# One level of Strassen's scheme in the MLP of a two-block model kernel, in two phases with sums that pass through DRAM

## The reference, cut to what matters

```
h  = h + m @ w_o                                   # [1024, 1024]
hn = rms_norm(h, norm2_g)
gate, up = split(hn @ w_gate_up)                   # w_gate_up [1024, 2 * 2816]
x  = rms_norm(h + (silu(gate) * up) @ w_down, final_g)   # w_down [2816, 1024]
h2 = rms_norm_2(x, pre_norm_g)                     # the second block goes on from here
```

## Time and profile before

| | |
|---|---|
| median of 3 runs | 2475.63 us (2475.03 to 2477.4) |
| span of the profiled execution | 2474.4 us |
| TensorE busy, mean granted clock | 2305.9 us (93%), 0.971 |
| VectorE, ScalarE, GpSimd busy | 1235.1, 774.9, 804.8 us |
| bytes moved by DMA | 135.97 MB, mean 55 GB/s |

### The profile page before, as it was taken

One profiled execution on the slowest core, in us unless ns is written; L12 is line 12 of the kernel. 1 busy time (PEld: TensorE's weight loads), 2 busy tenths in 40 slices (PEclk: granted clock), 3 DMA queues, 4 the chain that ended last, 5 costly groups with the idle time before them and its releaser, 6 DMA issues.

```text
span 2474.4 us, 30540 instructions
## 1 busy us (share of the span) xinstructions
PE 2305.9 (93%) x11208; PEld 1902.4 (77%) x11208; DVE 1235.1 (50%) x2685; ACT 774.9 (31%) x1327; POOL 804.8 (33%) x380
## 2 busy tenths in 40 slices
PE   6999999999997789999899999999999789998896
PEld 6876788988885677878688888888888577787875
DVE  3368899999304678220433333333333544506723
ACT  5245422332224455022411111111111442226632
POOL 1355433555432121223432222323232532230032
PEclk9999999999998799999999999999999799999998
DMA  3211112111132000422111111111111031110122
GB/s 104 58 52 65 55 43 56 52 35 52 52 98 65 26 9 1 168 62 78 35 52 42 51 42 51 42 51 46 48 51 43 26 120 52 43 43 22 54 71 85
DMA packets 178082, 135.97 MB, mean 55 GB/s; under 512 B 4529, under 2 KB 163918, under 8 KB 177982
## 3 DMA queue, kind: packets, MB, share of 16 engines
q1 hardware_dynamic: 173990, 121.48, 16.4%
q10 hardware_dynamic: 3992, 13.11, 1.3%
HBM read 116.87 MB, written 16.78 MB: 54 GB/s over the span
## 4 chain that ended last, share of the span: by engine, by line
PE 74%; DVE 8%; ACT 3%; POOL 2%; issue 2%; DMA 0%; ACTq 0%; DVEq 0%; POOLq 0%
PE ps L705 27%; PE ps L914 19%; PE ps L931 9%; PE ps L977 8%; PE ps L1123 3%; PE ps L813 2%; PE ps L834 2%; PE ps L846 2%; DVE logit L1768 1%; ACT p_s L1582 1%; POOL n_acc L2318 1%; DVE logit L1755 1%; PE ps L871 1%; POOL x_lo L2346 1%; PE ps L1046 0%
## 5 line engine op out<-in xcount | busy, mean ns | idle before, releaser
L2137 POOL TENSOR_TENSOR w_lo<-w_raw,w_hi 128x1024 fp32r<-128x1024 f32 (+1 forms) x127 | 276.1, 2175 | 898.9 <-ACT w_hi L1155 898.9
L705 PE MATMUL ps<-x_hi,w_hi 128*128 128x512 f32 (+2 forms) x1200 | 455.4, 379 | 8.3 <-DVE c_rs L1673 3.3
L705 PE MATMUL ps<-x_lo,w_hi 128*128 128x512 f32 (+2 forms) x1200 | 452.4, 377 | 0.0
L705 PE MATMUL ps<-x_hi,w_lo 128*128 128x512 f32 (+2 forms) x1200 | 450.4, 375 | 0.0
L2294 POOL TENSOR_TENSOR w_lo<-w_raw,w_hi 128x1024 fp32r<-128x1024 f32 x66 | 158.9, 2408 | 504.0 <-ACT w_hi L1444 504.0
L914 PE MATMUL ps<-x_hi,w_hi 128*128 128x512 f32 x704 | 277.9, 395 | 2.5 <-POOL x_lo L2278 2.5
L914 PE MATMUL ps<-x_lo,w_hi 128*128 128x512 f32 x704 | 279.1, 396 | 0.0
L914 PE MATMUL ps<-x_hi,w_lo 128*128 128x512 f32 x704 | 277.5, 394 | 0.0
L705 PEld LDWEIGHTS ps<-x_hi,w_hi 128*128 128x128 f32 x1200 | 228.0, 190 | 52.7 <-issue 11.5
L705 PEld LDWEIGHTS ps<-x_hi,w_lo 128*128 128x128 f32 x1200 | 227.8, 190 | 37.2
L705 PEld LDWEIGHTS ps<-x_lo,w_hi 128*128 128x128 f32 x1200 | 227.7, 190 | 36.2
(11 more groups left out here) (341 smaller groups left out, 4075.4 us busy)
## 6 DMA issues: line engine op xcount, KB each, us to landing
w_raw<-in_w_in SPq DMA_DIRECT2D x74, 512.0 KB, 3.7
w_raw<-in_w_gate_up SPq DMA_DIRECT2D x44, 512.0 KB, 3.8
w_raw<-in_w_down SPq DMA_DIRECT2D x22, 512.0 KB, 3.5
q_scratch<-stage ACTq DMA_DIRECT2D x8, 512.0 KB, 2.6
g_scratch<-g_ring ACTq DMA_DIRECT2D x8, 512.0 KB, 2.7
q_f<-q_scratch SPq DMA_DIRECT2D x8, 512.0 KB, 4.1
w_raw<-in_w_b SPq DMA_DIRECT2D x8, 512.0 KB, 5.0
g_s<-g_scratch SPq DMA_DIRECT2D x8, 512.0 KB, 3.7
```

Of the source, the lines that this page charges most:

```text
L705: mm = pe.matmul(ps[:, b, 0:n], w[:, s, P * k:P * k + P], r[:, k, t0:t0 + n], start=k == 0 and i == 0, stop=k == kd - 1 and i == 2 and ext ...
L2137: pool.tensor_tensor(w_lo[:, p % 2, 0:n], w_raw[:, p % 2, 0:n], w_hi[:, p % 2, 0:n], ALU.subtract).then_inc(wlo_done, 1)
```

## The change

The MLP is done in two phases. Activations and weights are cut in halves: activations by model width (m 0 to 3, m 4 to 7) and by token half, the gate and up panels of a chunk by model width, so that gate and up for both token halves are a 2x2 by 2x2 block product. One level of Strassen's scheme (in Winograd's form) makes it from seven products P1 to P7 in place of eight; a product is one 128x512 bank, 4 k-steps of 3 matmuls.

Phase 1: `strassen_pair(n)`, n from 0 to 21, with 84 matmuls each. VectorE makes the weight sums (`combined_weights`, 4 instructions per chunk), the output sums (`gate_up_pair`, 5) and, in every second pair, sums of two chunks' inner activations (`inner_sums`, 4). GpSimd makes sums of the down weights (`down_combined`, 4 per two chunks). Inner sums (7 x 256 KB per two chunks) and down-weight sums (4 x 256 KB) are stored to DRAM. The residual `mix` is stored to DRAM as `h_scratch` (4 MB), since its place holds the normalised activations and their sums; VectorE waits for these stores (`hs_store`) before it normalises in place.

Phase 2: `down_step(s)`, s from 0 to 76: seven products (p) of 11 steps (j), each with 12 matmuls into four banks. Each step loads 256 KB of weights and 256 KB of inner activations, ScalarE casts both, VectorE and GpSimd take one low part each. Banks change sides with each product, and `down_sums` and `with_residual` sum the seven into `mix`. `h_scratch` is loaded back from step 14 on. Squares for the next norm are taken for finished tiles from the fifth product on; four tiles of 128x512 are left for the end.

The loops of the MLP are written out instead of being loops of the chip. The diff, cut to its core:

```diff
             def norm_sums(i):
-                pe.wait_ge(acca_done, 7 * i + 7)
                 if i:
-                    pe.wait_ge(accb_done, 7)
-                    pe.wait_ge(upper_free, 2 * KD + 16 * (FC - 1))
+                    pe.wait_ge(acc2a_done, 14)
+                    pe.wait_ge(acc2b_done, 14)
+                    pe.wait_ge(dn_done, 28)
+                else:
+                    pe.wait_ge(acca_done, 7)
...
-            def gate_and_up(it, par, first=False, between=None):
-            def down(it, par, off, chunks=1):
...
+            def strassen_pair(n):
+                at = 4 * (n % 2)
+                for i, prod in enumerate(products(n)):
+                    q = 7 * n + i
+                    pe.wait_ge(*low_w(q))
+                    if prod == "P2":
+                        pe.wait_ge(r1_done, n + 1)
+                    if prod == "P7":
+                        pe.wait_ge(po_done, 5 * n + 1)
+                    if prod == "P3":
+                        pe.wait_ge(po_done, 5 * n + 3)
...
+                    b = at + {"P1": 0, "P2": 0, "P6": 1, "P7": 1, "P5": 2, "P3": 2, "P4": 3}[prod]
+                    for k in range(4):
+                        if n == 0:
+                            pe.wait_ge(*low_x(4 * i + k))
+                        for e, (w, r) in enumerate(((wr_hi, xb_hi), (wr_hi, xb_lo), (wr_lo, xb_hi))):
+                            mm = pe.matmul(ps[:, b, :], w[:, q % SLOTS, P * k:P * k + P], r[prod][:, k, :],
...
+            def down_step(s):
+                p, j = s // HJ, s % HJ
+                pe.wait_ge(*low_w(M2 + s))
+                pe.wait_ge(*low_s(s))
+                for f in range(4):
...
+                    for e, (w, r) in enumerate(((wr_hi, sr_hi), (wr_hi, sr_lo), (wr_lo, sr_hi))):
+                        mm = pe.matmul(ps[:, 4 * (p % 2) + f, :], w[:, (M2 + s) % SLOTS, P * f:P * f + P], r[s % SLOTS][:, :],
...
+            sp.wait_ge(h_done, 2 * KD)
+            load_pair(1)
+            for m in range(KD):
+                sp.dma_start(h_scratch[m], mix[:, m, :]).then_inc(hs_store, 16)
...
+            for s in range(STEPS):
...
+                if s >= 4:
+                    sp.wait_ge(*low_w(M2 + s - 4))
+                sp.dma_start(block_source(M2 + s), down_weights(p, j)).then_inc(wst_load[s % 4], 16)
...
+                if s >= 4:
+                    sp.wait_ge(*low_s(s - 4))
+                if s == 8:
+                    store_inner(HJ - 1)
...
+                sp.dma_start(wdr[:, s % 4, :], as_scratch[p, j]).then_inc(sst_load[s % 4], 16)
+                if 14 <= s < 14 + KD:
...
+                    sp.dma_start(mix[:, s - 14, :], h_scratch[s - 14]).then_inc(h_load, 16)
...
+            dve.wait_ge(hs_store, 16 * KD)
+            for z in range(8):
+                normalized(z)
+            for y in (1, 3):
+                x_low(y)
...
+            def gate_up_pair(n):
+                if n + 1 < FC:
+                    combined_weights(n + 1)
+                for i in range(7):
+                    if i == at("P6"):
...
+                        dve.tensor_tensor(a[0][:, :], r1[:, :], ps[:, b + 1, :], ALU.add).then_inc(po_done, 1)
+                    if i == at("P7"):
...
+                        dve.tensor_tensor(g1[:, :], r1[:, :], ps[:, b + 1, :], ALU.add).then_inc(po_done, 1)
+                        dve.wait_ge(po_done, done + 2)
+                        dve.tensor_tensor(a[1][:, :], g1[:, :], ps[:, b + 2, :], ALU.add).then_inc(po_done, 1)
...
+                    block_low(q + SLOTS)
+                    if i == 2 and n >= 2 and n % 2 == 0:
+                        inner_sums(n // 2 - 1)
...
+            def block_high(q):
...
+                    act.wait_ge(tw_done, TW_DONE_0 + 4 * n + 4)
+                if q >= SLOTS:
+                    act.wait_ge(blk_done, BLK_DONE_0 + q - SLOTS + 1)
+                act.copy(wr_hi[:, q % SLOTS, :], block_source(q)).then_inc(wh_done, 1)
...
+            def final_squares(z):
+                m, h = FINAL[z]
+                act.wait_ge(dn_done, 9 + z if z < 4 else 11 + 2 * (z - 3) if z < 8 else 13 + z)
+                for st in range(2):
+                    if z >= 3:
+                        act.wait_ge(acc2b_done if st else acc2a_done, added(z - 2))
+                    dst = n_acc2[:, st, half(h)] if z in (0, 4) else n_sq2[st][:, z % 2, :]
+                    act.activation(dst, mix[:, m, half(h)], ACT.Square, scale=v("final_g", m) if st else 1.0).then_inc(sq2_done, 1)
```

More of the change, by code:

```diff
@@ L954, in _ @@
             pe.wait_ge(h_done, 2 * KD)
-            gate_and_up(0, 0, first=True)
-            with pe.Fori(0, (FC - 2) // 2) as it:
-                for par in range(2):
-                    gate_and_up(it, par + 1)
-                    down(it, par, 3 * par + 4)
-            it_last = (FC - 2) // 2
-            gate_and_up(it_last, 1, between=memory_turned)
+            for n in range(FC):
+                strassen_pair(n)
+            for s in range(STEPS):
+                down_step(s)
+                if s == 6 * HJ + 4:
+                    memory_turned()
             pe.wait_ge(memlo_done, MEMLO_0 + KD)
-            down(it_last, 0, 4, chunks=2)
             def linear(key, j, rhs_hi, rhs_lo, t0, n):
@@ L1473, in _ @@
-            it_last = (FC - 2) // 2
-            activations(it_last, 1, between=memory_high_parts)
-            for m in range(KD):
-                act.wait_ge(upper_free, 2 * KD + 16 * (FC - 2) + 2 * m + 2)
-                squares(1, m)
-            split_mlp(it_last, 6, L2)
-            split_mlp(it_last, 7, L2)
-            norm(1)
+                squares(m)
+                if m == KD - 2:
+                    for q in range(SLOTS):
+                        block_high(q)
+            norm_split()
@@ L1484, in v_panel @@
+            for z in range(12, 16):
+                final_squares(z)
+            norm()
             def v_panel(m):
@@ L1878, in sums @@
-            def sums(it, par, at, behind=None):
-                for n in range(16):
-                    m, (t0, w) = n // 2, HALF[n % 2]
-                    dve.wait_ge(lin_full, at + (n + 1))
-                    dve.wait_ge(upper_free, 32 * it + (16 * par + n + 2 * KD - 7))
-                    dve.tensor_tensor(mix[:, m, t0:t0 + w], mix[:, m, t0:t0 + w], ps[:, 4 + n % 4, :], ALU.add).then_inc(upper_free, 1)
-                    if behind is not None and n % 2:
-                        behind(m - 1)
@@ new lines, in _ @@
+            for z in range(8, 12):
+                normalized(z)
+            for y in (5, 7):
+                x_low(y)
+            for z in range(12, 16):
+                normalized(z)
+            for y in (9, 11):
+                x_low(y)
+            for k in range(4):
+                dve.wait_ge(hn_done, HN_DONE_0 + 12 + k + 1)
+                dve.wait_ge(xh_done, 8 + k + 1)
+                dve.wait_ge(*low_x(8 + k))
+                dve.tensor_tensor(mix[:, 4 + k, half(1)], mix[:, 4 + k, half(1)], mix[:, k, half(1)], ALU.add).then_inc(s0_done, 1)
@@ L1925, in _ @@
+            for z in range(12, 16):
+                final_sums(z)
             dve.wait_ge(stat_full, 2)
@@ L2303, in _ @@
-            activations(0, 0, first=True)
+            for q in range(0, SLOTS, 2):
+                block_low(q)
+            for y in range(0, 28, 2):
+                prod, k = FIRST[y // 4], y % 4
+                pool.wait_ge(xh_done, y + 1)
+                src = {"P1": mix[:, k, half(0)], "P2": mix[:, 4 + k, half(0)], "P4": mix[:, 4 + k, half(1)], "P5": mix[:, 4 + k, half(1)],
+                       "P6": wdr[:, k, :], "P7": mix[:, k, half(1)], "P3": mix[:, 4 + k, half(0)]}[prod]
+                pool.tensor_tensor(xb_lo[prod][:, k, :], src, xb_hi[prod][:, k, :], ALU.subtract).then_inc(xl_even, 1)
@@ new lines, in final_sums @@
+            def final_sums(z):
+                if z in (0, 4):
+                    return
+                m, h = FINAL[z]
+                pool.wait_ge(sq2_done, 2 * z + 2)
+                if added(z) > 1:
+                    pool.wait_ge(acc2b_done, added(z) - 1)
+                pool.tensor_tensor(n_acc2[:, 1, half(h)], n_acc2[:, 1, half(h)], n_sq2[1][:, z % 2, :], ALU.add).then_inc(acc2b_done, 1)
+            for s in range(STEPS):
+                p, j = s // HJ, s % HJ
+                block_low(M2 + s + SLOTS)
+                inner_low(s + SLOTS)
+                if p >= 3 and j == 1:
+                    with_residual(p)
+                if p >= 4 and 2 <= j < 6:
+                    final_sums(4 * (p - 4) + j - 2)
+                if s == 6 * HJ + 8:
+                    split(AT2[PANELS2[0]])
+                    split(AT2[PANELS2[1]])
@@ L2307, in _ @@
                                pattern=[[0, 4], [-1, P]], channel_multiplier=1).then_inc(wsp_done, 1)
[L2308 to L2323 removed]
+            low_parts()
             for m in range(2):
```

642 lines of the change are left out of this document (440 added, 202 removed).

## The result

The changed kernel takes 2419.34 us (median of 4 runs, 2417.67 to 2421.43) against 2476.22 us (4 runs) for the kernel before: ratio 0.9769, 95% interval 0.9755 to 0.9783, so 57 us less. The forecast was 2410 us; the range 2398 to 2438 holds the result, the own range of the likeliest case, 2403 to 2420, ended 0.7 us above it. The profiled execution took 2417.67 us, its span is 2415.9 us (forecast 2408.7), the mean granted clock 0.962 (0.971 before).

A forecast was written before the change was run, and what follows sets the result against it. In the MLP only matmuls count, at their starting distance on TensorE. Matmuls -91.9, start +33.6, end waits -5.4 and squares -2.0 give -65.7 us: span 2408.7, plus 1.2 to the median, 2410 us; range 2398 to 2438.

The forecast's parts named there:

- the likeliest case: The forecast of 2410 us itself, without any rival: chance 0.62, own range 2403 to 2420 us.
- The matmuls: MLP: 2772 matmuls in place of 3168, 396 fewer at 232.1 ns each, -91.9 us if TensorE stays fed.
- The store: Ahead of the norm: VectorE's first scaling waits for the store of h, starting at 1202.3 us (between 1200.2 and 1213.4).
- The first pair: VectorE's list delays P7 to 1246.3 us, at the low clock; 84 matmuls end at 1255, 33.6 us later than before.
- the sign: First pair: TensorE idle some 15 us ahead of its first P7, ended by VectorE's first output sum.
- All fit: Other 21 pairs, 19.5 us each: VectorE's 11 to 16 us, GpSimd's 13 to 16 and ScalarE's 10 x 0.6 fit.
- The steady pairs: Other 21 pairs: P7-to-P3 handoff costs 0.1 us per pair, 2 us in all, bounds 0 and 15.
- The second phase: 77 steps of 2.79 us, 214.8 us, with loads and other engines hidden; 1.75 us of transposes counted besides.
- B: Rival: second phase bound by bytes at 200 GB/s, 243 us, 28 more than 215, so 2438 us; chance 0.09.
- C: Rival: each second-phase step's two loads served in turn, 5.2 us per step against 2.79, so 2596 us; chance 0.04.
- The end: After the last matmul: GpSimd's four additions of squares end at 8.5 us, before 10.5; partition sums start at 1890.8 us.

The follow-up runs named there:

- the third experiment: Changed kernel with h stored tile by tile along with the output projection's loads, and the second chunk's weights loaded last: 2410.24 us, ratio 0.9733.
- The second experiment: Changed kernel with GpSimd's first four down-weight sums moved one pair later, from the first pair to the second: 2407.64 us, ratio 0.9725.
- the last experiment: Kernel with the first output sum ahead, plus all additions of squares of the last four tiles on VectorE, none on GpSimd: 2399.88 us, ratio 0.9690.
- the last three kernels: On the three moves, cumulatively: low parts of P5 and P6 on VectorE (2401.31 us), first output sum ahead of weight sums (2405.47), tail squares on VectorE (2399.88).
- the three moves: Changed kernel with copy of P1 early, first down-weight sums one pair later, and h stored along with the output projection: 2400.70 us, ratio 0.9694.
- the four edits: The three moves plus all 28 low parts of activations on VectorE, none on GpSimd; together against the kernel before the change: 2405.49 us, ratio 0.9708.

## Why the prediction was right, and where 9 us went

**The matmuls.** Right. 396 fewer; the distance is 130.37 / 561 = 232.4 ns, a little above the 231.7 used for the first phase, which makes 1764 x 0.7 ns = 1.2 us.

**The store.** Right: forecast 1202.3, measured 1203.41, and 1200.5 to 1202.6 in the kernels with the same code ahead of it. It costs what was said, and the third experiment shows that it need not cost anything.

**The first pair.** The sum came out (P7 at 1246.96 for 1246.3, the next pair at 1254.39 for 1255), by luck; the mechanism was wrong. I read the earlier trace rows as both engines slowing each other in SBUF all along, VectorE by 0.5 us per instruction of GpSimd, 6 us in all. In the trace VectorE lost 1.1 us in each of two low parts, 1.0 us in each of two weight sums and 0.3 us in a low part of weights, 4.4 us, and nothing in its run of additions from 1218.5 to 1235.4 us, in which GpSimd's stood still. Its low parts of activations were done by 1234 where I had about 1240, also since its instructions follow each other at 0.60 to 0.66 us, not at 0.688. And it was not what P7 waited for. TensorE had not run P2, P4, P5 and P6 in between: P2 waited for ScalarE's copy of P1, in a queue that I had not read, and with that gone, P5 waits for GpSimd. The four products ran from 1233.06 to 1246.1 us, and P7 waited 0.88 us for the sum behind them; the idle time of some 15 us ahead of P7 that I had named as the sign did not come. Two errors cancelled: a list on VectorE that I took too long, and products that ran late. P7 also did not start at the low clock: after 0.88 us of idle it ran at 1.00. The low clock had been paid before it, in P1 and from 1233.06 to 1236.6.

**The second pair.** Here the forecast failed, at the sentence "All fit" on the other 21 pairs: it was true of a steady pair, and applied to the second, where GpSimd comes out of the start late. Its low part of weights at 1247.09, done at 1248.39, releases SyncE, whose next issues (chunk 2, then down weights) wait in its queue; the down weights land at 1257.9; GpSimd's four sums stand ahead of its next low parts of weights; those free the slot for chunk 2's sums on VectorE, which stand ahead of the output sum that P7 needs. The price: waits of 1.74 and 4.57 us, and behind them 12 matmuls at 0.427 us, 2.3 us more, at half the clock (0.54 from 1272.29 to 1278.00): 8.6 us. Counted from the start of one matmul to the start of the next, which is what TensorE loses, it is 1.9, 4.7 and 2.5 us, 9.1 in all. The second experiment takes the down-weight sums out, both waits and the low clock behind them are gone from its trace, and 9.4 us come back between the two points (10.9 by the medians), so this is shown.

**The steady pairs.** Right, better than forecast: no stall in place of 2 us. The fit is not slack: without P4 between P7 and P3 the handoff costs 1.84 us per pair.

**The second phase.** Right: 216.49 us for 214.8 + 1.75 = 216.55. B and C are refuted by 359 GB/s without a lost matmul. (The pieces of h are 512 KB, not a quarter of 1 MB as the prediction has it for the whole phase; no sum rests on that.)

**The end.** 9.3 us for 8.5. I had counted GpSimd's four additions of squares; the chain runs through VectorE's four, which take 1.56 to 1.60 us each beside GpSimd's (0.68 without them, in the last experiment).

The ledger against the forecast of 1890.8 for the partition sums: first pair -0.6, second pair +9.1, rate +1.2, no stalls -2.0, end +0.8, and +0.2 that I can't place: +8.7, so 1899.5. Behind it the program is 1.5 us shorter than before. The other 2.2 us of the 9.3 between forecast and median lie between span and median of the runs, 3.4 us where I took 1.2; the profiled execution was the shortest of the four.

**Why it stops at 2400.** In the last three kernels and in the one with the three moves the time from the first scaling to the second phase is 460.1 to 461.8 us. 1848 x 0.2324 = 429.5 of it are matmuls, so about 31 us of start are left. What the first pair waits for longest is another thing in each: GpSimd's low part ahead of P5 (14.37 us) with the three moves, VectorE's first output sum ahead of P7 (11.63 us) with the low parts of P5 and P6 moved, GpSimd's low part and VectorE's later sums (4.32 and 5.88 us) with the first sum ahead. Up to the low parts of the second pair's weights VectorE's list is about 41 us long in the first two of them. That VectorE and GpSimd together can't prepare the first pair sooner in this order is my reading of the traces, not shown; a kernel with a shorter list, such as one that spreads the activation sums over the first products, was not run.

## What to carry to other kernels

When a change turns a pipelined start into a burst of preparation, price the first two rounds with each engine's queue in its written order, not with its busy time: here the wait that looked largest (19.79 us) was worth 2 us, and four additions of one pair too early were worth 10. Put one-time transfers where their queue idles anyway, even if the consumer is far away. And try gains together: of the four edits that helped or might have, three added up and the fourth turned to nothing, since it removed the same waits as one of the three.

## What the runs showed of the hardware

- Additions with both operands in SBUF on both engines at once are not shared evenly. While VectorE issued them back to back at 0.61 us, one GpSimd addition took 15.47 us and ended 1.1 us behind the first gap in VectorE's run, one of 0.03 us at 1235.44; its group in the changed kernel (shortest, median and longest in ns):

```profile
L2612 POOL TENSOR_TENSOR xl_P<-mix,xh_P x12: 1267/1292/15468, 1204.9 to 1245.9; 128x512 fp32r<-128x512 f32 x12
```

  The other way round, VectorE's took 1.56 to 1.76 us in place of 0.68 in two low parts (1209.28, 1214.20), two weight sums (1235.47, 1237.16) and the last additions of squares, all beside an addition of GpSimd. VectorE's scalings, which have one operand in PSUM, took 0.74 us each beside GpSimd's low parts, and those took 1.27 to 1.29 us (1204.88 to 1208.79). What decides who goes first was not isolated.
- The granted clock was at the lower level (0.50) in P1 of the changed kernel, behind 7.48 us of idle, and fell to it (windows of 0.55 and 0.54) behind idle times of 19.79 and 4.57 us; it stayed at 1.00 behind 0.88, 1.55 and 1.74 us, and, with P3 right behind P7, through twenty-one idle times of 1.6 us, one per pair.
- SyncE's eight stores of 512 KB took 8.83 us to issue one behind the other, 1.1 us each (0.43 to 1.51). The same stores issued 13 us apart, along with the output projection, took 0.32 to 0.34 us each, all but the first.
